# Second kind of layer: the 28 gate and decay columns ride along in the fox value product, and four steps change places

## The reference, cut to what matters

```
h = rms_norm_2(x, norm_g)
z = h @ w_in                                   # 256 tokens x 3612 columns
(fq, fk, fv, ff, f_gate, glu_in, c_gate,
 nq, nkc, nvc, nks, nvs, nkw, nvw, n_gl, n_gate) = jnp.split(z, split_points, axis=-1)
o_a = fox_attention(fq, fk, fv, ff + fox_b) * jax.nn.silu(f_gate)
o_b = conformer_conv(glu_in, ...) * jax.nn.silu(c_gate)
o_c = nsa_attention(nq, ..., n_gl, ...) * jax.nn.silu(n_gate)
return x + jnp.concatenate([o_a, o_b, o_c], axis=-1) @ w_out

# in fox_attention: c = cumsum(log_sigmoid(f_logit), axis=1), added to the scores
# in nsa_attention: gates = sigmoid(gate_logit), one per head and branch
```

## Time and profile before

| | |
|---|---|
| median of 3 runs | 1565.98 us (1565.82 to 1566.51) |
| the profiled execution: its time | 1565.87 us |
| the profiled execution: its span, first to last instruction | 1564.0 us |
| TensorE busy | 1548.2 us |
| VectorE busy | 1031.7 us |
| ScalarE busy | 815.4 us |
| GpSimd busy | 243.8 us |
| DMA | 274.12 MB, mean 175 GB/s |

### The profile page before, as it was taken

The page is one execution under the profiler, slowest core; times in us unless marked ns, Lnnn a source line. Parts: engine busy times, 40 slices in busy tenths (PEclk is TensorE's granted clock), DMA queues, the critical chain, the costliest instruction groups (busy, mean ns, idle before and its releaser), DMA issues.

```text
span 1564.0 us, 27149 instructions
## 1 busy us (share of the span) xinstructions
PE 1548.2 (99%) x11188; PEld 1407.1 (90%) x11188; DVE 1031.7 (66%) x1241; ACT 815.4 (52%) x1119; POOL 243.8 (16%) x207
## 2 busy tenths in 40 slices
PE   9999999999999999999999999999999999999998
PEld 8999988898989999999998889998999998979886
DVE  4655567876765555655556786686555578977796
ACT  5444455754454434544445675445443464756484
POOL 0000061010000000000006101000000019802970
PEclk9999999999999999999999999999999999999999
DMA  8657655453555555565766445355565566145712
GB/s 256 221 188 206 215 172 163 129 162 109 189 186 192 188 191 187 162 216 187 217 204 184 153 128 166 118 175 189 189 202 198 164 223 216 62 142 189 242 35 94
DMA packets 210036, 274.12 MB, mean 175 GB/s; under 512 B 21046, under 2 KB 170392, under 8 KB 209432
## 3 DMA queue, kind: packets, MB, share of 16 engines
q1 hardware_dynamic: 209800, 272.82, 54.4%
q10 hardware_dynamic: 144, 0.00, 0.0%
HBM read 271.75 MB, written 1.08 MB: 174 GB/s over the span
## 4 chain that ended last, share of the span: by engine, by line
PE 90%; DVE 5%; ACT 1%; DMA 1%; issue 1%; SPq 1%; POOL 0%; POOLq 0%; ACTq 0%; DVEq 0%
PE bank L579 29%; PE bank L628 14%; PE bank L1077 10%; PE bank L1066 7%; PE bank L2192 4%; PE bank L1281 4%; PE bank L2170 3%; PE bank L2441 3%; PE bank L1377 3%; PE bank L1223 1%; DMA raw<-in_ffn_w 1%; PE bank L1048 1%; DVE G L2740 1%; DVE wlo L489 1%; PE bank L1154 1%
## 5 line engine op out<-in xcount | busy, mean ns | idle before, releaser
L489 DVE TENSOR_TENSOR wlo<-raw,whi 128x2048 fp32r<-128x2048 f32 (+1 forms) x247 | 559.1, 2267 | 305.4 <-ACT whi L478 305.1
L478 ACT ACTIVATE whi<-raw 128x2048 fp32r<-128x2048 f32 (+2 forms) x249 | 467.5, 1880 | 261.8 <-PE bank L628 102.0
L579 PE MATMUL bank<-hT_hi,whi 128*128 128x256 f32 x1408 | 391.6, 278 | 2.3 <-DVE wlo L452 1.3
L579 PE MATMUL bank<-hT_lo,whi 128*128 128x256 f32 x1408 | 389.6, 277 | 0.0
L579 PE MATMUL bank<-hT_hi,wlo 128*128 128x256 f32 x1408 | 389.4, 277 | 0.0
L579 PEld LDWEIGHTS bank<-hT_hi,whi 128*128 128x128 f32 x1408 | 264.3, 188 | 4.7 <-DVE wlo L452 1.7
L579 PEld LDWEIGHTS bank<-hT_lo,whi 128*128 128x128 f32 x1408 | 265.0, 188 | 0.0
L579 PEld LDWEIGHTS bank<-hT_hi,wlo 128*128 128x128 f32 x1408 | 264.3, 188 | 0.0
L628 PE MATMUL bank<-whi,Y 128*128 128x512 f32 (+1 forms) x748 | 224.7, 377 | 0.0
L628 PEld LDWEIGHTS bank<-whi,Y 128*128 128x128 f32 x748 | 140.1, 188 | 27.8
L330 POOL TENSOR_TENSOR st<-st 128x1 f32<-128x1 f32 x17 | 14.1, 834 | 915.3 <-ACT X L323 915.3
(11 more groups left out here) (411 smaller groups left out, 2718.5 us busy)
## 6 DMA issues: line engine op xcount, KB each, us to landing
raw<-in_ffn_w SPq DMA_DIRECT2D x131, 1024.0 KB, 5.3
raw<-in_w_in SPq DMA_DIRECT2D x80, 1024.0 KB, 5.3
raw<-in_w_out SPq DMA_DIRECT2D x16, 1024.0 KB, 4.9
raw<-in_w_br_na SPq DMA_DIRECT2D x4, 1024.0 KB, 5.0
raw<-in_w_br_mla SPq DMA_DIRECT2D x4, 1024.0 KB, 5.1
raw<-in_w_br_gla SPq DMA_DIRECT2D x4, 1024.0 KB, 5.0
Y<-rpb_line SPq DMA_DIRECT2D x4, 868.5 KB, 10.8
raw<-in_mla_w_ukv SPq DMA_DIRECT2D x2, 1024.0 KB, 5.5
```

Of the source, the lines that this page charges most:

```text
L478: act.activation(m["whi"][:, slot, 0:w], m["raw"][:, slot, 0:w], ACT.Copy).then_inc(s.hi_ready, 1)
L489: dve.tensor_tensor(m["wlo"][:, slot, 0:w], m["raw"][:, slot, 0:w], m["whi"][:, slot, 0:w].bitcast(F32), ALU.subtract).then_inc(s.lo_ready, 1)
L579: mm = pe.matmul(B[bank][:, mt * T:(mt + 1) * T], a, b, start=(n == 0 and k == 0), stop=(n == KK - 1 and k == 2))
```

## The change

The 28 columns move into the first product. Unit 0 becomes seven of the eight row blocks of a 284 column wide matrix (256 of fv, 4 of ff, 24 of n_gl), unit 1 the eighth. The 48 products of `fv` now have 284 moving columns, the first token tile goes to bank 7 and the second to bank 1. The 24 products of `sm` are gone. ScalarE copies the four ff columns out to `ffc`, applies the tanh to the 24 others, and copies fv, all in its step `fv`, which now stands between hi.3 and hi.4. TensorE turns the two ff tiles (`ff`, two transposes with 128 moving columns) after tall.0, and VectorE's `sm` reads that result. The two transposes of `sg` are gone. ScalarE's `params` waits for the last product of `fv`, as both use bank 1.

Four steps change places: VectorE's lo.1 goes from ahead of hl.15 to ahead of hl.8; the first value product is cut into two, one half ahead of `cmp_kt` and one behind; ScalarE's copy turn.9 goes ahead of exp.13; and at the start of the program two more roundings of activations go ahead of the first half unit, on ScalarE and on VectorE.

```diff
-                if i in (1, 7):
+                if i in (3, 7):
                     ring.act_first(act, i // 4)
...
-                if i in (1, 7):
+                if i in (3, 7):
                     ring.dve_first(dve, i // 4)
...
 PE2 = words("""
-    fv.0-5 params fv.6 xt.1 fv.7-15 sm tall.0 tall.3-4 tall.1-2 sg w1.0-1 scores.0 tok.1 tok_b.1 w1.2-3 tok.0
-    turn.0-1 hid_fold turn.2 tok_b.0 tall.5 cmp_kv heads_turn cmp_kt value.0 cmp_score scores.1 tall.6 cmp_turn.0 scores.2 cmp_turn.1
+    fv.0-5 params fv.6 xt.1 fv.7-15 tall.0 ff tall.3-4 tall.1-2 w1.0-1 scores.0 tok.1 tok_b.1 w1.2-3 tok.0
+    turn.0-1 hid_fold turn.2 tok_b.0 tall.5 cmp_kv heads_turn fox_value.0 cmp_kt fox_value.1 cmp_score scores.1 tall.6 cmp_turn.0 scores.2 cmp_turn.1
     tall.7 turn.3 scores.3 turn.4-5 tall.8 turn.6-7 scores.4 ln.0 turn.8 value.1 turn.9 ln.1 value.2 ln.2 turn.10-11 wo.0-2
     turn.12 wo.3 pw turn.13 wo.8-9 turn.14 wo.10 value.3-4 wo.11 wo.4-6 wo.12-13 wo.7 wo.14 wo_a.15 xt_next wo_b.15
 """)
 ACT2 = words("""
-    hh.0-5 sq.1 hh.6-15 hi.2 params hi.3 sm hi.4 decay tall.0 hi.5 fox_own tall.4 hi.6 tall.1 hi.7 tall.2 hi.8 exp.0-2
-    hi.9 fv hi.10 tok_b.1 hid_out hi.11 turn.0-2 hi.12 gelu tok_b.0 tall.5 heads_turn hi.13 hi.14
+    hh.0-5 sq.1 hh.6-15 hi.2 params hi.3 fv hi.4 decay tall.0 hi.5 fox_own tall.4 hi.6 tall.1 hi.7 tall.2 hi.8 exp.0-2
+    hi.9-10 tok_b.1 hid_out hi.11 turn.0-2 hi.12 gelu tok_b.0 tall.5 heads_turn hi.13 hi.14
     cmp_prob exp.3-5 tall.6 cmp_turn.0-1 prob.1 exp.6-8 hi.15 tall.7 turn.3-5 prob.2 exp.9-11 out.0 hi.16 turn.6 hi.17
-    ln_square tall.8 turn.7 exp.12 turn.8 exp.13 turn.9 exp.14 ln_tanh turn.10-11 out.1 ln_high hi.18 turn.12-14 hi.19
+    ln_square tall.8 turn.7 exp.12 turn.8-9 exp.13-14 ln_tanh turn.10-11 out.1 ln_high hi.18 turn.12-14 hi.19
     conv_out hi.20 out.2
 """)
 DVE2 = words("""
-    hl.4-6 scale.1 hl.7-14 lo.1 hl.15 lo.2-3 sm lo.4 decay tall.0 lo.5 blk.0-1 tall.4 cmp_zero taps.0 lo.6
-    fox_bias taps.1 lo.7 taps.2-3 sg lo.8 peak.0-2 prob.0 lo.9 taps.4-5 lo.10 taps.6 lo.11 gelu gelu_out lo.12
+    hl.4-6 scale.1 hl.7 lo.1 hl.8-15 lo.2-3 sg sm lo.4 decay tall.0 lo.5 blk.0-1 tall.4 cmp_zero taps.0 lo.6
+    fox_bias taps.1 lo.7 taps.2-3 lo.8 peak.0-2 prob.0 lo.9 taps.4-5 lo.10 taps.6 lo.11 gelu gelu_out lo.12
     rotate cmp_kv cmp_score tall.5 taps.7 cmp_shift peak.3-5 cmp_prob lo.13 tall.6 prob.1
     peak.6-8 taps.8-9 lo.14 prob.2 taps.10 peak.9 taps.11-12 peak.10 taps.13 peak.11 taps.14-15 out.0 tall.7 prob.3 ln.0 peak.12
     out_low.0 tall.8 peak.13 ln.1 peak.14 lo.15 ln.2 out.1 prob.4 ln_silu lo.16 ln_split lo.17 out_low.1 lo.18 conv_out
     conv_low out.2 lo.19 out_low.2 lo.20
 """)
-UNITS2 = {"tok": 1, "tok_b": 1, "tall": 1, "sm": 1, "pw": 1}
+UNITS2 = {"tok": 1, "tok_b": 1, "tall": 1, "pw": 1}
+FV = 284
+FV_ROWS = (7, 1)
...
-        n = {("fv", 0): 1, ("wo", 0): 1, ("wo", 4): 1, ("wo", 8): 1, ("wo", 12): 1}.get(step, UNITS2.get(step[0], 0))
+        n = {("fv", 0): 2, ("wo", 0): 1, ("wo", 4): 1, ("wo", 8): 1, ("wo", 12): 1}.get(step, UNITS2.get(step[0], 0))
         at += n
-        width += [{"sm": 224, "pw": 512}.get(step[0], UNIT)] * n
-        dmas += [2 if step[0] == "sm" else 1] * n
+        width += [rows * FV for rows in FV_ROWS] if step == ("fv", 0) else [{"pw": 512}.get(step[0], UNIT)] * n
+        dmas += [2 if step == ("fv", 0) else 1] * n
     return first, width, dmas
...
-            elif step == "sm":
-                ring.load_beside(sp, u, 28, (0, w_in[:, :, 768:772]), (4, w_in[:, :, 3076:3100]))
             elif (step, i) == ("fv", 0):
-                ring.load(sp, u, (whole, w_in[:, :, 512:768]))
+                for h, (a, b) in enumerate(((0, 7), (7, 8))):
+                    ring.load_beside(sp, u + h, FV, (0, w_in[:, a:b, 512:772]), (260, w_in[:, a:b, 3076:3100]))
...
+                pe.wait_ge(s.tall_out, past.tall_out + 1)
...
-        def sg_turn():
+        def ff_turn():
 
             pe.wait_ge(s.small_out, past.small_out + 1)
-            pe.wait_ge(s.ff_in, past.ff_in + 1)
             for t in range(NT):
-                mm = pe.transpose(B[3][:, T + t * 28:T + (t + 1) * 28], small_T[:, t * P:(t + 1) * P], ident[0:28, 0:28])
-            mm.then_inc(s.sgT_done, 1)
+                mm = pe.transpose(B[3][0:4, t * P:(t + 1) * P], ffc[:, t], ident)
+            mm.then_inc(s.ffT_done, 1)
 
         def fox_v(n):
 
             t, kk = n // KK, K_ORDER[n % KK]
-            slot = wait_unit(unit(("fv", 0)))
+            slot = wait_unit(unit(("fv", 0)) + kk // 7)
             norm.pe_wait(pe, n0, t, kk)
-            for k, (a, b) in enumerate(passes(hT(kk, t * P, P), ring.w(slot, kk * 256, 256))):
-                mm = pe.matmul(B[7][:, t * T:(t + 1) * T], a, b, start=(n % KK == 0 and k == 0), stop=(n % KK == 7 and k == 2))
-            if n == 15:
+            for k, (a, b) in enumerate(passes(hT(kk, t * P, P), ring.w(slot, kk % 7 * FV, FV))):
+                mm = pe.matmul(B[FV_BANK[t]][:, 0:FV], a, b, start=(n % KK == 0 and k == 0), stop=(n % KK == 7 and k == 2))
+            if n >= 14:
                 mm.then_inc(s.unit_used, 1)
 
         def params():
 
             pe.wait_ge(s.params_in, past.params_in + 16 * N_PARAMS2)
             for i in range(2):
-                pe.transpose(B[1][:, 34 * i:34 * i + 34], conv_rows[:, i * P:(i + 1) * P], ident[0:34, 0:34])
-            pe.transpose(B[1][:, 68:100], pe_rows, ident[0:32, 0:32]).then_inc(s.paramT_done, 1)
+                pe.transpose(B[1][:, FV + 34 * i:FV + 34 * i + 34], conv_rows[:, i * P:(i + 1) * P], ident[0:34, 0:34])
+            pe.transpose(B[1][:, FV + 68:FV + 100], pe_rows, ident[0:32, 0:32]).then_inc(s.paramT_done, 1)
...
+        def fox_value(i):
+
+            o = B[5][:, :].rearrange("p (i q) -> p i q", i=2)
+            pe.wait_ge(s.pT_ready, past.pT_ready + 3)
+            pe.wait_ge(s.tall_out, past.tall_out + 4)
+            for b in range(2):
+                h = 2 * i + b
+                pe.matmul(o[64 * b:64 * b + 64, i, :], fv[:, 0, h * HD:(h + 1) * HD], PT0[0][:, h, :], start=True, stop=False)
+                mm = pe.matmul(o[64 * b:64 * b + 64, i, P:T], fv[:, 1, h * HD:(h + 1) * HD], PT1[0][:, h, :], start=False, stop=True)
+            if i:
+                mm.then_inc(s.value_done, 1)
...
-        def sm():
-            u = unit(("sm", 0))
-            act.wait_ge(s.unit_used, u + 1)
-            act.activation(small_T, B[3][0:28, 0:T], ACT.Tanh, scale=0.5).then_inc(s.small_out, 1)
-
         def fox_v():
-            u = unit(("fv", 0))
-            act.wait_ge(s.unit_used, u + 1)
-            act.activation(X[:, 7680:8192], B[7][:, :], ACT.Copy).then_inc(s.tall_out, 1)
+            act.wait_ge(s.unit_used, unit(("fv", 0)) + 2)
+            for t in range(NT):
+                act.activation(ffc[:, t], B[FV_BANK[t]][:, 256:260], ACT.Copy)
+            for t in range(NT):
+                ins = act.activation(sg[:, 24 * t:24 * t + 24], B[FV_BANK[t]][:, 260:FV], ACT.Tanh, scale=0.5)
+            ins.then_inc(s.small_out, 1)
+            for t in range(NT):
+                ins = act.activation(fv[:, t], B[FV_BANK[t]][:, 0:256], ACT.Copy)
+            ins.then_inc(s.tall_out, 1)
 
         def params():
             act.wait_ge(s.paramT_done, past.paramT_done + 1)
-
-            act.activation(conv_p[:, :, 0:TAPS], B[1][:, 0:68].rearrange("p (i r) -> p i r", i=2)[:, :, 0:TAPS],
+            act.wait_ge(s.unit_used, unit(("fv", 0)) + 2)
...
         def sm():
-            dve.wait_ge(s.small_out, past.small_out + 1)
+            dve.wait_ge(s.ffT_done, past.ffT_done + 1)
             dve.wait_ge(s.params_in, past.params_in + 16 * N_PARAMS2)
             dve.tensor_scalar(ffT[0], B[3][0:4, 0:T], fox_b, None, ALU.add).then_inc(s.ff_in, 1)
 
         def sg_out():
-            dve.wait_ge(s.sgT_done, past.sgT_done + 1)
-            dve.tensor_scalar(sg.rearrange("p (t n) -> p t n", t=NT),
-                              B[3][:, T:T + 56].rearrange("p (t n) -> p t n", t=NT)[:, :, 4:28],
-                              1.0, 0.5, ALU.add, ALU.mult).then_inc(s.sg_ready, 1)
+            dve.wait_ge(s.small_out, past.small_out + 1)
+            dve.tensor_scalar(sg, sg, 1.0, 0.5, ALU.add, ALU.mult).then_inc(s.sg_ready, 1)
```

More of the change, by code:

```diff
@@ L2009 @@
 TOK_BANK = [(7, 0), (4, 5)]
+FV_BANK = (7, 1)
 OUT_BANK = (0, 1, 7, 2)
@@ L2057, in second_layer @@
     ffT = [X[0:4, 256 * k:256 * k + T] for k in range(3)]
-    small_T = X[0:28, 768:1024]
+    ffc = X[:, 768:776].rearrange("p (t n) -> p t n", t=NT)
     gates = G[:, 0:2048]
@@ L2135, in _ @@
                 load_w1(sp, W1_LOADS[step, i])
-            if (step, i) == ("sm", 0):
+            if (step, i) == ("fv", 0):
                 with nc.allow_non_contiguous_dma(reason="one float per partition"):
@@ L2295, in turn @@
                 pe.wait_ge(s.tok_out, past.tok_out + 1)
-                pe.wait_ge(s.sg_ready, past.sg_ready + 1)
+                pe.wait_ge(s.ff_in, past.ff_in + 1)
             if j == 3:
```

(25 more changed lines are left out.)

18 lines of the change are left out of this document (5 added, 13 removed).

## The result

| | median | lowest to highest | executions |
|---|---|---|---|
| before | 1566.16 us | 1564.68 to 1568.15 | 21 |
| after | 1568.73 us | 1566.38 to 1572.76 | 21 |

After stands to before as 1.0018, 95% interval 1.0011 to 1.0024: slower by 2.8 us (1.7 to 3.8). The forecast was 1566.0 us, range 1564.3 to 1567.9. The profiled execution of after took 1572.76 us (span 1570.9). It is the slowest of the 21, so its rows show the worst that this kernel does, not the middle.

What follows compares the result with a forecast made beforehand. TensorE, busy nearly the whole span, was taken as the bound. Terms of +0.5, -0.3 and zeros gave +0.2 us on the profiled 1565.87 us; the forecast was 1566.0 us, 8-in-10 range 1564.3 to 1567.9.

Steps and rivals of the forecast that it cites:

- TensorE now stands still for about 2.8 us: Ahead of tall.0: with `sm` gone, tall.0 keeps its start because it waits for lo.2, leaving about 2.8 us idle.
- The worth of the removal is 0: Removing the `sm` products gains 0, against 2.15 us per layer if the wait for lo.2 were not there.
- rival 3: Standstill ahead of tall.0 drops the clock to half rate: 1.65 us lost per layer, 1569.2 us; chance 0.08.
- What waits for ff: VectorE's `sm` waits for ff behind tall.0, making lo.6 late for TensorE by 0.5 us in the first layer.
- Rival 4: The ff wait exceeds its slack, lo.5 and lo.6 both late, 1.5 us per layer: 1568.9 us; chance 0.08.
- The pace of TensorE: Block of five `tall` units: ff sets the slow pace for four; layer totals, ff wait included, +0.5 and -0.3 us.
- The start: Start of program: the 0.58 us stall moves behind the half unit; worth 0, bounds -0.6 and 0.
- the value split: Fox value in two halves: the 0.68 us stall moves from `cmp_kt` to `cmp_score`; worth 0, bounds -0.68 and 0 per layer.
- the copies ahead of exponentials: value.2 still waits 0.38 us for the copy of turn.8; worth 0, bounds -0.38 and +0.4 per layer.
- The 0 for lo.1: VectorE's lo.1 ahead of hl.8: nothing on TensorE's path asks for it, worth 0.
- The paper gain (rival 1): lo.2 comes earlier and the stalls really close: 7.0 us gained, 1559.0 us; chance 0.04.
- The forecast's own sum of +0.2: Whole kernel: +0.5 and -0.3 for the two layers, 0 for the rest, giving +0.2 us.

Runs made afterwards that it cites:

- kernel 2: Before with 23 of the 24 `sm` products left out, opening a standstill ahead of tall.0; 1568.37 us, ratio 1.0017 to before.
- kernel 5: After with 9 filler products, whose result nobody reads, in the standstill ahead of tall.0; 1566.98 us, ratio 1.0008 to before.
- kernel 9: Before with ScalarE's hi.2 moved ahead of hh.8-15 and nothing else changed; 1565.61 us, ratio 1.0002 to before.
- kernel 3: Before with only the start-of-program move, the split fox value product and turn.9 ahead of exp.13; 1565.47 us, ratio 1.0002 to before.
- kernel 7: After with hi.2 ahead of hh.8-15, ff ahead of tall.0, ScalarE's fv ahead of params, sg and sm ahead of lo.3; 1562.86 us, ratio 0.9979 to before.
- kernel 8: Before with 12 of the 24 `sm` products left out; 1565.70 us, ratio 0.9995 to before.
- kernel 6: After with ff ahead of tall.0, ScalarE's fv directly behind hi.2, sg and sm ahead of lo.3; 1567.69 us, ratio 1.0009 to before.
- kernel 1: After with 22 filler products of the identity put ahead of tall.0; 1570.12 us, ratio 1.0034 to before.

## Why the prediction was wrong

**The step that failed** is "TensorE now stands still for about 2.8 us", followed by "The worth of the removal is 0". The first half was right: the standstill is 2.68 us, lo.2 ends it, and tall.0 starts 11.13 us (first layer) and 11.54 us (second) after the first `fv` product, in after as in before (the prediction had read 10.9 for before). The second half took for granted that tall.0 behind the standstill is the same tall.0. It is not: its clock falls in most executions, and the sum had no term for that. This is rival 3, to which I gave 0.08; `sm` had kept the clock up as well as the wait covered (kernels 2 and 5 from either side).

**The sum against the two profiled executions.** From the first `fv` product to the first w1 product the first layer went from 39.00 to 42.55 us: 3.0 of the 3.55 more are tall.0 at half clock, 0.6 are the wait in front of tall.2. The second went from 40.23 to 42.11 us: 2.9 more for tall.0, and 1.0 less, mostly because the other four units ran at the quick pace. Without the clock that is +0.6 and -1.0, where the prediction had +0.5 and -0.3. So the missing term is the clock. Of the 6.9 us between the two spans 5.4 lie here; 0.8 lie ahead of the first of these stretches, whose start varies between 1258.7 and 1260.5 us over all the profiled kernels, with and without the change.

**Why rival 3 was set so low.** I read the earlier trace rows as a sign that the clock does not fall for stops under 3 us: it shows 1.00 in the 3 us after the last product. That is one stop of one execution. The granted clock of after fell 2.0 us into the first standstill, in some executions it did not fall at all, and neither can be read from one stop. The rule I cited from the Trainium skill ("TensorE: Matmul & The Clock Gate", Part 1), that an idle TensorE loses its clock, spoke against the change, and the trace of after agrees with it (0.50 over 6.8 us, twice). As I cited it, it gives the direction alone. Which standstills cost is shown here by the runs: 1.4 us did not, 2.7 us did in most executions.

**Its price** was mis-sized per execution: 1.65 us per layer, against 3.0 (8.57 less 5.54) and 3.1 in the profiled execution, where half rate lasted 6.8 us instead of the 3.3 of the earlier trace rows. In kernel 2's profiled execution it lasted 3.4 us and cost 1.3 us (29.18 us from tall.0 to w1, 27.87 before), so this price was met there. The median of 1568.73 us lies near my 1569.2 us by luck, as it mixes executions with two long falls, with shorter ones and with none. That the slow loads of the earlier trace rows ran at 1.2 GHz was my reading of their durations; the granted clock of the profile shows 1.00 there.

**What waits for ff:** right in its size. 0.62 us in front of tall.2 in the first layer, forecast 0.5; no wait for lo.4 or lo.5. In kernel 5, where the clock stays up, it is 0.63 us. Rival 4 (a wait that runs away) did not come.

**The pace of TensorE:** wrong, though it cost little. I let ff decide for the slow pace. The second layer of after went at 21.79 / 192 = 0.1135 us, the quick one. The pace does not follow from TensorE's order of work: the five units of the second layer took 28.49 us in before and 27.20 us in kernel 9, whose TensorE order is the same. What sets it is open. The row of kernel 9:

```profile
1420.09 27.20 PE bank L2192 x240
```

**The start, the value split, the copies ahead of exponentials:** 0 for the three together was right (kernel 3); each by itself was not measured. At the start, unit 1 begins at 17.99 us, forecast 17.8; the stall moved behind the half unit. `cmp_score` comes 4.8 us behind the end of tall.5, forecast 4.5. The 0 for lo.1 was never tested alone.

**The paper gain (rival 1):** it was there to be had in part, but only with lo.2 made earlier and ff ahead of tall.0 (kernel 7), which this change does not do.

**What stays open.** The seven executions of after with a mean clock of 0.999 or 1.000, and kernel 5, lie 0.8 and 1.1 us over before. The forecast's own sum of +0.2 and the uncertainty of these comparisons (kernel 5: -0.2 to +2.7 us) can hold that, but no run here splits it. The wider products, the moved loads and the move of lo.1 were never tested alone; they stand in kernel 5 and could have a share in its 1.1 us. Nor is it settled what decides in which execution the clock falls.

## What to carry to other kernels

Before work is taken off a busy TensorE, look for the operand that the next product waits for: if it comes no earlier, the work was cover, and its removal opens a standstill. Here one of 1.4 us was free, and one of 2.7 us saved nothing and cost nearly 3 us, since the products behind it ran at half clock in at least 14 of 21 executions. Move the late operand first (here one rounding of 1.9 us, eight steps earlier in ScalarE's order), then take the cover away. Moving the rounding alone gave nothing, and taking the cover away alone lost time; both together, with the small turn that followed also moved into the short standstill that was left, gained 3 us. Look for a fall of the clock in short stretches: over the whole program the mean clock of an execution with a short one still read 0.999.

## What the runs showed of the hardware

- The granted clock can fall to 0.50 within a standstill of 2.7 us: the mean clock was under 0.999 in 14 of 21 executions of after and 7 of 11 of kernel 2 (at least 8 fell), and in none of 12 with a standstill of 1.4 us (kernel 8, where the profiled execution shows 1.00). In the profiled executions it fell 2.0 us into the first standstill of after and stayed at half rate for 6.8 us twice, and for 3.4 us once in kernel 2, over work that kept TensorE busy.
- 0.64 us and 1.66 us of standstill with two short transposes between them lost the clock in at least 6 of 11 executions (kernel 6).
- A plain 32-bit product of 128 by 128 by 128 is recorded as two of 0.11 us each (kernel 1).
- The same unbroken block of 240 products takes 27.2 to 28.5 us at full clock (0.1133 to 0.1187 us each), from one profiled execution to another and from one layer to the other, without a change in its work.
